# Another order for the indexer stage of the second block: rotations, values and gates, choice rounds and index tiles

## The reference, cut to what matters

```python
h = h + rmsnorm(y, norm_post[1])              # end of the first block
...
h = rmsnorm_2(x, norm_mix)                    # start of the second
proj = einsum('bsd,dc->bsc', h, w_in)         # qa, ka, va, qi, ki, wi, qb, kvb, gb, gates
qa, ka, qi, ki = rope(qa), rope(ka), rope(qi), rope(ki)
score = einsum('bth,bths->bts', wi, relu(einsum('bthd,bsd->bths', qi, ki)))   # the indexer
_, sel = top_k(where(causal, score, -inf), 128)                               # the choice
s = einsum('bthd,btkd->bthk', qa, ka[sel])    # then attention over the chosen keys
```

## Time and profile before

| | before |
|---|---|
| runs, us | 2733.94, 2728.93, 2733.46; median 2733.46 |
| profiled execution: its time, us | 2732.84 |
| its span, us | 2730.8 |
| busy in the span: PE / DVE / ACT / POOL | 88% / 62% / 48% / 30% |
| mean granted TensorE clock | 0.934 of full |
| last projection's last half starts again on PE | 1598.02 |
| px 4 starts on PE | 1639.97 |
| attention's first reduce on DVE | 1720.17 |
| last mask of the choice ready | 1793.34 |

### The profile page before, as it was taken

The page is one execution under the profiler, slowest core; times in us unless marked ns, Lnnn a source line. Parts: engine busy times, 40 slices in busy tenths (PEclk is TensorE's granted clock), DMA queues, the critical chain, the costliest instruction groups (busy, mean ns, idle before and its releaser), DMA issues.

```text
span 2730.8 us, 38619 instructions
## 1 busy us (share of the span) xinstructions
PE 2395.4 (88%) x15931; PEld 2126.6 (78%) x15931; DVE 1691.7 (62%) x2599; ACT 1305.5 (48%) x2125; POOL 821.8 (30%) x505
## 2 busy tenths in 40 slices
PE   4999997889899999999998987888888883999994
PEld 3999996888899889899897775567666673777873
DVE  3455545778843766666665656856556414888885
ACT  3434434344432555565565333442344212888884
POOL 1211113455431222222221110213110113776772
PEclk8999998899999999999998989998899986999997
DMA  4222420100052222222222331124110432778873
GB/s 144 79 81 89 129 78 32 32 32 32 13 142 70 63 78 78 71 76 64 75 68 53 88 92 31 47 54 121 43 43 12 154 104 81 284 282 286 291 263 146
DMA packets 226601, 273.43 MB, mean 100 GB/s; under 512 B 42089, under 2 KB 194250, under 8 KB 213755
## 3 DMA queue, kind: packets, MB, share of 16 engines
q1 hardware_dynamic: 211914, 262.54, 30.5%
q0 software_dynamic: 14512, 8.45, 1.0%
HBM read 283.24 MB, written 31.05 MB: 115 GB/s over the span
## 4 chain that ended last, share of the span: by engine, by line
PE 53%; DVE 22%; ACT 12%; POOL 6%; issue 5%; DMA 2%; SPq 1%; DVEq 0%; POOLq 0%; ACTq 0%
PE ps L92 16%; PE ps L93 14%; PE ps L94 14%; ACT whi L98 2%; DVE prods L1145 2%; ACT sp L114 1%; PE ps L1821 1%; DVE fsum L972 1%; DVE wlo L102 1%; DVE work L2711 1%; DVE p L2116 1%; POOL xg L3880 1%; DVE m L2709 1%; ACT X L114 1%; PE ps L1831 1%
## 5 line engine op out<-in xcount | busy, mean ns | idle before, releaser
L92 PE MATMUL ps<-hn_h,whi 128*128 128x264 f32 (+2 forms) x2256 | 692.1, 307 | 39.2 <-POOL wlo L102 30.1
L93 PE MATMUL ps<-hn_l,whi 128*128 128x264 f32 (+2 forms) x2256 | 674.5, 299 | 0.0
L94 PE MATMUL ps<-hn_h,wlo 128*128 128x264 f32 (+2 forms) x2256 | 674.4, 299 | 0.0
L92 PEld LDWEIGHTS ps<-hn_h,whi 128*128 128x128 f32 x2256 | 430.9, 191 | 68.7 <-issue 37.8
L94 PEld LDWEIGHTS ps<-hn_h,wlo 128*128 128x128 f32 x2256 | 431.4, 191 | 12.4
L93 PEld LDWEIGHTS ps<-hn_l,whi 128*128 128x128 f32 x2256 | 431.5, 191 | 9.8 <-issue 0.2
L102 POOL TENSOR_TENSOR wlo<-wraw,whi 128x2048 fp32r<-128x2048 f32 (+1 forms) x46 | 167.7, 3645 | 567.0 <-ACT whi L98 567.0
L98 ACT ACTIVATE whi<-wraw 128x2048 fp32r<-128x2048 f32 (+1 forms) x164 | 260.0, 1586 | 63.0 <-PE ps L94 62.4
L102 DVE TENSOR_TENSOR wlo<-wraw,whi 128x2048 fp32r<-128x2048 f32 (+1 forms) x118 | 249.5, 2115 | 49.9 <-ACT whi L98 49.2
L732 DVE SCALAR_TENSOR_TENSOR c<-ub,vec,c 128x528 f32<-128x528 f32 x48 | 45.3, 943 | 140.7 <-ACT c L114 140.7
L114 ACT ACTIVATE ub<-ps,vec 128x528 f32<-128x528 f32 x48 | 33.7, 702 | 165.9 <-PE ps L94 165.9
(11 more groups left out here) (772 smaller groups left out, 6771.4 us busy)
## 6 DMA issues: line engine op xcount, KB each, us to landing
wraw<-in_w_gate_up SPq DMA_DIRECT2D x33, 1024.0 KB
wraw<-in_hy_w_in SPq DMA_DIRECT2D x32, 1024.0 KB, 5.6
wraw<-in_da_w_in SPq DMA_DIRECT2D x64, 512.0 KB, 4.2
ex_raw<-in_w_gate_up SPq DMA_DIRECT2D x31, 1024.0 KB
ex_raw<-in_w_down SPq DMA_DIRECT2D x17, 1024.0 KB
wraw<-in_w_down SPq DMA_DIRECT2D x15, 1024.0 KB
wraw<-in_w_in SPq DMA_DIRECT2D x14, 1024.0 KB, 5.4
wraw<-in_hy_w_out SPq DMA_DIRECT2D x8, 1024.0 KB, 8.6
```

The lines of the kernel that those rows point to most:

```text
L92: e.matmul(out, lhsT=l[0], rhs=r[0], start=start, stop=False)
L93: e.matmul(out, lhsT=l[0], rhs=r[1], start=False, stop=False)
L94: return e.matmul(out, lhsT=l[1], rhs=r[0], start=False, stop=stop)
```

## The change

Nothing is computed in another way; what changes is the order, and one engine.

- `lo_by`: the low part of `ka` moves from DVE to POOL. It stood on DVE between z = 0 and z = 1; it now stands on POOL behind the tree of sums.
- `weights_beside`: at m = 6 of the last projection the engines now split up to `vgw`, one chunk more than before.
- In `vector_mix` the tile (7, 1) and the norm's second root each come one k later; the low part of `qa1` goes from ahead of the list to behind `parts` 3.
- `tensor_project`, px 4: the columns' sum goes from k = 0 to k = 4, the rotations 0 to 2 from k = 3, 5, 6 to k = 5, 6, 7, the root's broadcast from k = 4 to k = 5.
- `MIX`: the three rotations come ahead of `vg`; each index tile moves up one projection or ahead of the parts beside it; the choice becomes an entry of its own and stands ahead of the `rot` (and of its wait) instead of behind it, five times three rounds as before.

```diff
@@ -250,7 +250,7 @@
 
         pool = i in even_slots if i >= EX else i % 3 == 0 and i != DAO + 1
         if first["vgw"] <= i < first["cmp"]:
-            pool = i == first["ki"] or i > first["gate", "a", 0]
+            pool = i in (first["ki"], first["ka"]) or i > first["gate", "a", 0]
         return ("w.lo.pool", i) if pool and not gathered(i) else ("w.lo.vec", i)
 
     def raw_of(i):
@@ -2208,6 +2208,10 @@
     def all_split(w):
         w.wait_ge("dao.vec", "lo", 15)
 
+    def weights_beside(m):
+
+        return first["dao", m] + 1 if m < 6 else first["vgw"] if m == 6 else first["ki"]
+
     def sync_dao(e, w):
         sync_weights(e, w, first["dao", 0] + 2)
         all_split(w)
@@ -2254,7 +2258,7 @@
     def scalar_dao(e, w):
         all_split(w)
         for m in range(8):
-            scalar_weights(e, w, first["dao", m] + 1 if m < 7 else first["ki"])
+            scalar_weights(e, w, weights_beside(m))
             if m == 5:
                 act(e, st2[:, 8:9], eps6, ACT.Sqrt).then_inc(*mark("dao.act", "table"))
             scalar_dao_squares(e, w, m, 0 if m == 7 else None)
@@ -2281,7 +2285,7 @@
     def vector_dao(e, w):
         all_split(w)
         for m in range(8):
-            lo_weights(e, w, "vec", first["dao", m] + 1 if m < 7 else first["ki"])
+            lo_weights(e, w, "vec", weights_beside(m))
             if m == 0:
                 w.wait_ge("pos")
                 e.tensor_copy(pf[:], pi[:]).then_inc(*mark("vec"))
@@ -2318,7 +2322,7 @@
             for h in range(2):
                 ts(e, to[:, :, h, :], by[:, :, 1 - h, :], -1.0, None, ALU.mult).then_inc(*mark("dao.pool", "swaps"))
         for m in range(8):
-            lo_weights(e, w, "pool", first["dao", m] + 1 if m < 7 else first["ki"])
+            lo_weights(e, w, "pool", weights_beside(m))
             if m in (1, 3):
                 w.wait_ge("dao.act", "sin", m)
                 ts(e, tabs[:, m, :], tabs[:, m, :], frq[:, m:m + 1], None, ALU.mult).then_inc(*mark("dao.pool", "table", m))
@@ -2475,13 +2479,13 @@
         else:
             left(w, x - 2)
         for k in range(8):
-            if (x, k) == (4, 0):
+            if x == 4 and k > 4:
+                tensor_rotation(e, w, k - 5)
+            if (x, k) == (4, 4):
                 w.wait_ge("n2.vec", "acc")
                 w.wait_ge("n2.pool", "acc")
                 tensor_columns(e, sq8b[:, 0], range(4)).then_inc(*mark("n2.pe", "sum"))
-            if x == 4 and k in (3, 5, 6):
-                tensor_rotation(e, w, k // 2 - 1 if k < 6 else 2)
-            if (x, k) == (4, 4):
+            if (x, k) == (4, 5):
                 w.wait_ge("n2.vec", "r")
                 tensor_along(e, bank[7], by_n2, range(4)).then_inc(*mark("n2.pe", "r"))
             tensor_project_part(e, w, x, k)
@@ -2565,7 +2569,7 @@
 
     def vector_project(e, w, x):
         rot = PX[x][2]
-        if x > 3:
+        if x > 4:
             lo_weights(e, w, "vec", first[PX[x][0]] + 1)
         if x < 9:
             return
@@ -2750,10 +2754,11 @@
                 *(mark(name, "tree", n // 2) if n > 1 else mark(name, "acc")))
 
 
-    MIX = [("px", 4), ("vg",), ("rot", 0), ("rot", 1), ("rot", 2), ("tables",), ("parts", 3), ("ix", 1, 0), ("ix", 1, 1),
-           ("px", 5), ("turn", 3), ("rot", 3), ("parts", 4), ("px", 6), ("turn", 4), ("rot", 4), ("ix", 2, 0), ("ix", 2, 1), ("parts", 5),
-           ("px", 7), ("turn", 5), ("rot", 5), ("ix", 3, 0), ("ix", 3, 1), ("parts", 6), ("px", 8), ("turn", 6), ("rot", 6), ("parts", 7),
-           ("turn", 7), ("rot", 7)]
+    MIX = [("px", 4), ("rot", 0), ("rot", 1), ("rot", 2), ("vg",), ("tables",), ("ix", 1, 0), ("ix", 1, 1), ("parts", 3), ("choose", 3),
+           ("px", 5), ("turn", 3), ("rot", 3), ("ix", 2, 0), ("ix", 2, 1), ("parts", 4), ("choose", 3),
+           ("px", 6), ("turn", 4), ("rot", 4), ("parts", 5), ("ix", 3, 0), ("ix", 3, 1), ("choose", 3),
+           ("px", 7), ("turn", 5), ("rot", 5), ("parts", 6), ("choose", 3),
+           ("px", 8), ("turn", 6), ("rot", 6), ("parts", 7), ("turn", 7), ("choose", 3), ("rot", 7)]
 
     def sync_mix(e, w):
         for kind, *of in MIX:
@@ -2803,20 +2808,17 @@
         for z in range(2):
             for k in range(8):
                 vector_mix_step(e, w, z, k)
-                if (z, k) == (0, 0):
+                if (z, k) == (0, 1):
                     vector_dao_tile(e, w, 7, 1)
-                if (z, k) == (0, 2):
+                if (z, k) == (0, 3):
                     vector_p1_root(e, w, 1)
             vector_mix_low(e, w, z, 7)
-            if z == 0:
-                lo_weights(e, w, "vec", first["ka"])
         mix_tree(e, w, "n2.vec", 1, add)
         vector_parts(e, w, 0)
         w.wait_ge("n2.act", "sqrt")
         e.reciprocal(by_n2, by_n2).then_inc(*mark("n2.vec", "r"))
         vector_parts(e, w, 1)
         vector_parts(e, w, 2)
-        lo_weights(e, w, "vec", first["qa1"])
         for kind, *of in MIX:
             if kind == "px":
                 vector_project(e, w, *of)
@@ -2824,18 +2826,21 @@
                 vector_turn_vg(e, w)
             elif kind == "parts":
                 vector_parts(e, w, *of)
+                if of[0] == 3:
+                    lo_weights(e, w, "vec", first["qa1"])
             elif kind == "tables":
                 for t in range(2):
                     e.scalar_tensor_tensor(tabs_r[:, t, :], tabs[:, t, :], 1.0, rr2[:], ALU.mult, ALU.mult).then_inc(*mark("n2.vec", "table", t))
             elif kind == "rot":
                 vector_rotated(e, w, *of)
-                if of[0] >= 3:
-                    vector_choose(e, w, 3)
+            elif kind == "choose":
+                vector_choose(e, w, *of)
             elif kind == "ix":
                 vector_index(e, w, *of)
 
     def gpsimd_mix(e, w):
         mix_tree(e, w, "n2.pool", 0, lambda e, out, a, b: e.tensor_tensor(out, a, b, ALU.add))
+        lo_weights(e, w, "pool", first["ka"])
         for kind, *of in MIX:
             if kind == "px":
                 gpsimd_project(e, w, *of)
```

## The result

| | before | after |
|---|---|---|
| median of the runs compared, us | 2732.62 | 2704.15 |
| range | 2728.93 to 2733.94 | 2701.3 to 2704.72 |
| profiled execution: time / span | 2732.84 / 2730.8 | 2704.6 / 2702.6 |

The ratio is 0.9896 with a 95% interval of 0.9879 to 0.9913: 28.5 us faster. The same kernel, run again five times beside eleven runs of the kernel before, gave 2704.26 against 2729.53, a ratio of 0.9906 (0.9892 to 0.992): 25.3 us between the medians.

The account below looks back on a forecast made before the run. No engine bounds the kernel up to attention; hand-overs between engines do. 4.7 us ahead of px 4 plus 18.3 in the list minus 1.5 for the clock made 21.5, forecasting 2712; own range 2709 to 2716, whole 2705 to 2722.

Parts of the forecast that it names:

- the clock in the first part: Ahead of px 4: low granted clock costs up to 8 us, some recoverable by shorter idle; counted as none.
- The term for the stretch ahead of px 4: From 1598 to px 4: 6.4 us gained on PE, of which 4.7 arrive because POOL blocks DVE.
- rival D: Between 1598 and 1635 the clock also recovers: 3 to 5 us more, 2707 to 2709; chance 0.12.
- vgw a tile sooner: Ahead of 1598: vgw's earlier split brings ki's load forward, so the sum ends 2.1 us sooner; bounds 0 and 4.2.
- The first k and the tile (7, 1): After 1598: tile (7, 1) no longer delays the first low part; PE's wait falls from 3.36 to 1.2, gaining 2.2 us.
- the root: Norm's second root one k later: PE's 1.72 us wait and part of DVE's go, gaining 2.1 us.
- ka on POOL: At z = 1: DVE loses a 3.41 us instruction, but POOL blocks its additions; 4.7 of 6.4 us arrive.
- The list: From px 4 to attention: DVE's waits fall from 25.6 to 7.3 us, gaining 18.3, less 1.5 charged for the clock.
- E: DVE idle filled before 1720 returns as idle between 1720 and 1793: no change within 0.2% (5.5 us); chance 0.03.
- C: In attention, late first gate chunks make PE or POOL wait, losing 5 to 10 us: 2717 to 2722; chance 0.06.
- A: In the list, turns 4 to 7 come late: 6 to 8 us more waits, 2718 to 2720; chance 0.2.
- B: TensorE stays at the low clock level through the list: slower, 2735 to about 2745; chance 0.02.

Follow-up runs that it names:

- e3_busy: Kernel before plus 30, 24 and 12 matmuls with unread results in PE's three idle stretches ahead of px 4; 2727.11 us against 2728.68, ratio 0.9988.
- e12_after_again: The changed kernel itself, run again five times and profiled a second time; 2704.26 us against 2729.53, ratio 0.9906.
- e1_front: Kernel before with only the edits ahead of px 4, old list behind; 2719.67 us against 2728.68, ratio 0.9964.
- e2_list: Kernel before with only the edits from px 4 on, old order ahead of it; 2711.24 us, ratio 0.9923.
- e4_after_busy: Changed kernel plus 15 and 8 matmuls with unread results in PE's two idle stretches left at the end of the last projection; 2703.65 us.
- e5_vgw: Kernel before with vgw split at m = 6 alone; dao 7's low part to the columns' sum 18.2 us, against 20.0 to 21.0 without the edit.
- e6_tile: Kernel before with tile (7, 1) and the root one k later, alone; columns' sum to px 4 36.8 us against 39.0 to 41.8; total 2741.85.
- e7_ka: Kernel before with ka's low part on POOL, alone; columns' sum to px 4 42.4 us against 41.8.
- e10_vec: Changed kernel with ki's and ka's low parts back on DVE, ka's behind z = 1; 2700.26 us against 2704.26 for the changed kernel beside it.

## Why the prediction was wrong

**The step that failed** is the clock in the first part: "In the first part the clock can give ... I count none." The term for the stretch ahead of px 4 was 4.7 us; between the two profiles it is 62.2 - 53.8 = 8.4. Order alone, at an equal granted clock of 1.00, is e3_busy's 56.6 against 52.3 and 52.2: 4.3 us. So the 4.7 was well sized for what it counted. The other 4.1 go with the clock: it cost the kernel before 62.2 - 56.6 = 5.6 us in the profile I read and the changed one 53.8 - 52.3 = 1.5. This is rival D, which had a chance of 0.12 and 3 to 5 us. Between these two profiles its mechanism and size came true, though the time lies below its 2707 too, by the drift told next. I had the row that pointed to it, the 0.80, and had worked out up to 8 us from it; to put the term at nothing had no row behind it.

**The rest of the miss** is the yardstick. The profiles' spans differ by 28.2 us: 1.7 ahead of every edit (dao 7's low part starts at 1575.89 instead of 1577.62), 8.4 to px 4, 17.3 in the list, 0.1 in attention up to the mask and 0.6 behind it, which with rounding is all. The 1.7 and the 0.6 are drift, not the change: the same instruction, with nothing changed ahead of it, starts between 1570.3 and 1577.6 us in the profiles of this case. And the untouched stage of 62.2 was the slowest of four, median 60.3. With the median of every stage (a 60.3 against 53.8, the latter from after, e12_after_again and e1_front; b 81.5 over the six old lists against 62.7 from after, e2_list, e4_after_busy and e12_after_again) the front gives 6.5 and the list 18.8. That is 25.3 in all, as much as between the medians of the second set of runs. By this yardstick the clock's share ahead of px 4 is 3.7 - 1.5 = 2.2 us, and 2.0 us more come in the list, where three of the six old ones had the long turn and the profile I read the short one. So the term that I put at nothing measured 2 to 4 us; that it is above nothing doesn't hang on the yardstick, its size does.

Step by step:

- vgw a tile sooner, 2.1: right. 2.2 in the changed kernel and about as much in e5_vgw, and blocked as worked out.
- The first k and the tile (7, 1), 2.2, and the root, 2.1: right in mechanism (waits of 1.3 and 0.4 instead of 3.4 and 1.7, e6_tile). How much of each reaches px 4 no run measured at an equal clock.
- ka on POOL costs 1.7 of 6.4: right in mechanism, about right in size. Counted from the start of POOL's tree, the three blocked additions and the low part end within 0.3 us of the forecast, and PE gets its two late tiles 0.5 and 0.7 us sooner than forecast. e7_ka shows that nothing is gained, and e10_vec gets 1.5 us of it back.
- px 4's start: forecast 1635, measured 1629.7, or 1631.4 without the drift ahead of the edits. The missing 3.9 us are about the clock's 4.1.
- The list, 18.3 less 1.5 for the clock: right, 17.3. DVE's waits are 8.8, not 7.3. Of the three turns without slack one, turn 6, was late, by 1.6 us. It wasn't slow itself (1.02 us a half), as I had charged it; the matmuls of px 7 ahead of it were, in a stretch granted 0.63 (1670 to 1674 us). In e12_after_again DVE waits for no turn longer than 0.5 us, so that this came to the 1.5 charged is in part luck. Turn 7, after 2.61 us idle, ran at the high level.
- Attention carries all of it: right, 73.11 against 73.17; E and C did not come about. Nor did A, which had 6 to 8 us more of waits than my 7.3, where 8.8 were measured, nor B: TensorE was granted 0.95 in the list, where it had 0.85 before.

What stays open is when the granted clock falls. The same stage, untouched, was granted 0.80, 0.86, 0.88 and 0.88 in four profiles, and no run here tells which of them the next execution gets.

## What to carry to other kernels

Price an idle stretch on TensorE twice where a chain handed from engine to engine goes through PE: once for its length and once for the matmuls behind it, which here took nearly twice as long (2.08 us for 1.13). Over one stage that came to 3.5 to 5.7 us. An edit that shortens the waits can get both back.

Read a stage that the change doesn't touch in more than one profile before its length is used as a yardstick. Here it moved by 2 us, with 4.7 us forecast for it.

And when an in-order engine waits at fixed places in its list, work that needs nothing, moved ahead of such a wait, fills it only as far as the wait reaches and the next producers aren't late in their turn. Five blocks of three rounds (2.83 us each) gave 7 to 9 us, where 11 were expected.

## What the runs showed of the hardware

- A vector instruction with both inputs in SBUF and a GpSimd instruction that reads SBUF wait for each other in whole instructions, in both directions: 0.42 us became 2.18, and GpSimd's 2.34 became 3.71 behind VectorE's 2.28. The vector engine's products with an input in PSUM (L2728 of before) kept their 0.40 to 0.42 us throughout.
- After waits of 2.52 and 2.55 us at the same place in the same list TensorE's turn took 2.08 us in e1_front and 1.13 in the kernel before. The wait alone doesn't settle the clock; what ran ahead of it in these two kernels differs.
- The changed kernel's stage ahead of px 4 was 35.6 us at a granted 0.95 and 34.1 at 1.00 in two executions of the same program.
- Matmuls whose result nobody reads made a stage 3.5 to 5.7 us shorter in which no engine had less to do, with the granted clock at 1.00. That rests on the one profile of e3_busy; the time in the total moved by too little (0.9976 to 1.0) to carry it alone.
